# A two-block transformer kernel: the expert router by masking, and half of one small product moved behind the first expert products

## The reference, cut to what matters

```python
def hierarchical_moe(x, w_rg, b_rg, w_re, b_re, w_g, w_u, w_d):
    ...
    g_prob = jax.nn.softmax((xt @ w_rg).astype(jnp.float32) + b_rg.astype(jnp.float32), axis=-1)
    g_val, g_idx = lax.top_k(g_prob, 1)
    e_logit = ((xt @ w_re).astype(jnp.float32) + b_re.astype(jnp.float32)).reshape(n, N_GROUPS, EXPERTS_PER_GROUP)
    e_logit = jnp.take_along_axis(e_logit, g_idx[:, :, None], axis=1)[:, 0]
    e_prob = jax.nn.softmax(e_logit, axis=-1)
    e_val, e_idx = lax.top_k(e_prob, TOP_K_IN_GROUP)
    e_val = e_val / jnp.sum(e_val, axis=-1, keepdims=True)
    within = jnp.sum(jax.nn.one_hot(e_idx, EXPERTS_PER_GROUP, dtype=jnp.float32) * e_val[..., None], axis=1)
    comb = jax.nn.one_hot(g_idx[:, 0], N_GROUPS, dtype=jnp.float32)[:, :, None] * (g_val * within)[:, None, :]
    ...

def second_block(...):
    ...
        x = layer_norm(ALPHA * x + mix, ln1_g[i], ln1_b[i])
        ffn = hierarchical_moe(x, w_route_group[i], b_route_group[i], w_route_expert[i], ...)
        ple = jax.nn.sigmoid(x @ w_ple_gate[i]) * (p[i] @ w_ple[i])
        x = layer_norm(ALPHA * x + ffn + ple, ln2_g[i], ln2_b[i])
```

## Time and profile before

| | us |
|---|---|
| three runs | 1791.07, 1795.44, 1798.85 |
| median | 1795.44 |
| profiled execution, its span | 1793.8 |

### The profile page before, as it was taken

One profiled execution on the slowest core, in us unless ns is written; L12 is line 12 of the kernel. 1 busy time (PEld: TensorE's weight loads), 2 busy tenths in 40 slices (PEclk: granted clock), 3 DMA queues, 4 the chain that ended last, 5 costly groups with the idle time before them and its releaser, 6 DMA issues.

```text
span 1793.8 us, 26178 instructions
## 1 busy us (share of the span) xinstructions
PE 1637.8 (91%) x10696; PEld 1288.2 (72%) x10696; DVE 1084.7 (60%) x1540; ACT 745.7 (42%) x974; POOL 0.2 (0%) x4
## 2 busy tenths in 40 slices
PE   7999999999999999999999899868779989997776
PEld 6877799998877798998887676435368767653433
DVE  6966767877886768877587662221265965412124
ACT  4666444554546535454456541101044564211111
POOL 0000000000000000000000000000000000000000
PEclk9999999999999999999999999989889999899888
DMA  7543346554563445555643499999945427899996
GB/s 257 181 150 135 129 165 203 172 199 148 180 194 102 160 134 188 187 179 153 208 154 122 164 406 381 417 416 414 401 146 181 165 94 289 351 413 416 413 416 240
DMA packets 174272, 422.55 MB, mean 236 GB/s; under 512 B 15984, under 2 KB 68568, under 8 KB 157528
## 3 DMA queue, kind: packets, MB, share of 16 engines
q1 hardware_dynamic: 174168, 421.07, 64.3%
HBM read 419.99 MB, written 1.05 MB: 235 GB/s over the span
## 4 chain that ended last, share of the span: by engine, by line
PE 63%; DMA 15%; DVE 12%; SPq 4%; ACT 3%; issue 3%; DVEq 0%; ACTq 0%
PE lot L287 16%; PE lot L289 16%; PE lot L288 16%; DVE w_lo L257 4%; PE lot L2248 4%; DMA e_hi<-w_exp_up 3%; SPq L2145 3%; DMA two_e_gates<-w_exp_down 3%; DMA raw<-w_exp_up 2%; ACT w_hi L252 2%; DMA two_e_sqT<-w_exp_up 1%; DMA two_e_gates<-w_exp_up 1%; DMA e_lo<-w_exp_up 1%; PE lot L414 1%; DMA e_hi<-w_exp_down 1%
## 5 line engine op out<-in xcount | busy, mean ns | idle before, releaser
L257 DVE TENSOR_TENSOR w_lo<-raw,w_hi 128x2048 fp32r<-128x2048 f32 (+4 forms) x194 | 431.8, 2230 | 129.0 <-ACT w_hi L252 128.3
L252 ACT ACTIVATE w_hi<-raw 128x2048 fp32r<-128x2048 f32 (+4 forms) x194 | 361.5, 1867 | 152.1 <-PE lot L289 138.1
L287 PE MATMUL lot<-one_hT_hi,w_hi 128*128 128x256 f32 x704 | 199.3, 283 | 0.7 <-issue 0.7
L289 PE MATMUL lot<-one_hT_hi,w_lo 128*128 128x256 f32 x704 | 199.2, 283 | 0.0
L288 PE MATMUL lot<-one_hT_lo,w_hi 128*128 128x256 f32 x704 | 199.2, 283 | 0.0
L287 PE MATMUL lot<-w_hi,two_hT_hi 128*128 128x512 f32 (+1 forms) x448 | 178.9, 399 | 4.7 <-DVE two_hT_lo L380 3.1
L289 PE MATMUL lot<-w_hi,two_hT_lo 128*128 128x512 f32 (+1 forms) x448 | 174.0, 388 | 0.0
L288 PE MATMUL lot<-w_lo,two_hT_hi 128*128 128x512 f32 (+1 forms) x448 | 173.9, 388 | 0.0
L287 PE MATMUL lot<-w_hi,one_hT_hi 128*128 128x512 f32 (+2 forms) x384 | 149.3, 389 | 6.9 <-DVE w_lo L257 5.3
L289 PE MATMUL lot<-w_hi,one_hT_lo 128*128 128x512 f32 (+2 forms) x384 | 145.7, 380 | 0.0
L288 PE MATMUL lot<-w_lo,one_hT_hi 128*128 128x512 f32 (+2 forms) x384 | 145.6, 379 | 0.0
(11 more groups left out here) (431 smaller groups left out, 3256.1 us busy)
## 6 DMA issues: line engine op xcount, KB each, us to landing
raw<-w_in SPq DMA_DIRECT2D x78, 1024.0 KB, 5.0
raw<-ffn_w_up SPq DMA_DIRECT2D x44, 1024.0 KB, 5.1
raw<-ffn_w_down SPq DMA_DIRECT2D x22, 1024.0 KB, 5.0
raw<-w_out SPq DMA_DIRECT2D x16, 1024.0 KB, 5.7
raw<-w_exp_gate SPq DMA_DIRECT2D x14, 1024.0 KB, 18.3
raw<-w_exp_up SPq DMA_DIRECT2D x14, 1024.0 KB, 20.6
two_e_gates<-w_exp_up SPq DMA_DIRECT2D x12, 1024.0 KB, 19.3
e_hi<-w_exp_up SPq DMA_DIRECT2D x10, 1024.0 KB, 22.3
```

What stands on the lines that cost most here:

```text
L252: act.activation(K.hi[:, r, 0:n], self.raw(name)[:, 0:n], ACT.Copy).then_inc(K.sig["hi_ready"], 1)
L257: dve.tensor_tensor(K.lo[:, r, 0:n], self.raw(name)[:, 0:n], K.hi[:, r, 0:n].bitcast(F32), ALU.subtract).then_inc(K.sig["lo_ready"], 1)
L287: pe.matmul(out, a[0], b[0], start=start, stop=False)
L289: return pe.matmul(out, a[1], b[0], start=False, stop=stop)
```

## The change

In the router, the two searches within the group go. The group's search stays, but with is-greater as its last step, which marks the three groups that were not picked (`cold`). One step a tile adds -1e30 there to the 32 expert logits. The instruction `max` then gives the eight largest of a tile's 32 values; six of the eight are overwritten by a marker that no value equals, `match_replace` writes the marker over the two that are left, and one comparison with -2e38 gives the marks. The softmax works on 32 values and not on 8. The weights' arithmetic that needed `expert_exps` moves behind `E.rows(dve, 0)`.

On PE, `pl1` is cut by tiles: tile 0 stays ahead of the rank products, tile 1 moves behind the first gate products `E.hidden(pe, 0, 0, 0)`, and the semaphore is raised behind tile 1. On ACT, the copy of `pl1` moves behind the copies of the first gather.

```diff
--- before.py
+++ after.py
@@ -2851,16 +2851,19 @@
         ST.done(out_part(0, 1, 1), "wo01")
         out_part(1, 1, 1).then_inc(L.filled("wot1"), 1)
 
-        def second_products(c):
-            lot = L.claim(pe, f"pl{c}")
+        def second_products(c, tiles=range(T)):
+            lot = L.use[f"pl{c}"][0]
+            if tiles[0] == 0:
+                L.claim(pe, f"pl{c}")
             if c == 0:
                 pe.wait_ge(sig["wple_in"], sig.at("wple_in", 16))
                 both("pT")
-            for t in range(T):
+            for t in tiles:
                 for k in range(2):
                     last = pe.matmul(K.ps[lot][:, t, :], M.pT[:, k, t * P:(t + 1) * P],
                                      w_ple[:, k, c * 512:(c + 1) * 512], start=k == 0, stop=k == 1)
-            last.then_inc(L.filled(f"pl{c}"), 1)
+            if t == T - 1:
+                last.then_inc(L.filled(f"pl{c}"), 1)
 
         def route_tile(t):
 
@@ -2880,7 +2883,7 @@
         route_tile(0)
         transpose_tile(K, L, pe, K.x, "nTt1", 1, sig, "n1_normed")
         route_tile(1)
-        second_products(1)
+        second_products(1, (0,))
         pe.wait_ge(sig["selected"], sig.at("selected", 1))
         L.claim(pe, "rank")
         tri, ones = M.tri_r[:, 0:P], M.tri_r[:, P:2 * P]
@@ -2893,6 +2896,7 @@
         both("rt")
         E.gather(pe, 0)
         E.hidden(pe, 0, 0, 0)
+        second_products(1, (1,))
         both("rank")
         L.claim(pe, "count")
         out = K.ps[L.use["count"][0]]
@@ -3081,9 +3085,9 @@
         act.wait_ge(sig["group_shift"], sig.at("group_shift", 1))
         act.activation(M.r[:, 0, :, 0:N_G], M.r[:, 0, :, 0:N_G], ACT.Exp).then_inc(sig["group_exps"], 1)
         act.wait_ge(sig["expert_shift"], sig.at("expert_shift", 1))
-        act.activation(M.r[:, 3, :, :], M.r[:, 3, :, :], ACT.Exp).then_inc(sig["expert_exps"], 1)
+        act.activation(M.r32[:, :, :], M.r32[:, :, :], ACT.Exp).then_inc(sig["expert_exps"], 1)
+        E.act_pieces(act, 0)
         take("pl1", M.pl[:, 1, :, :], whole)
-        E.act_pieces(act, 0)
         E.silu(act, 0, 0)
         if QB == 1:
             E.act_pieces(act, 1)
@@ -3341,45 +3345,33 @@
            M.route_b[:, :].unsqueeze(1).to_broadcast([P, T, N_ROUTE]), ALU.add).then_inc(L.drained("rt"), 1)
         L.wait_drained(dve, "rt")
 
-        def first_of(out, v, top, index, n):
-
-            small = M.r[:, 7, :, 0:n]
-            link(tt(small, v, top.to_broadcast([P, T, n]), ALU.is_equal))
-            link(dve.scalar_tensor_tensor(small, small, -100.0, index.unsqueeze(1).to_broadcast([P, T, n]),
-                                          ALU.mult, ALU.add))
-            link(dve.tensor_reduce(st[:, 146:148], small, AX_X, ALU.min))
-            link(tt(out, small, st[:, 146:148].unsqueeze(2).to_broadcast([P, T, n]), ALU.is_equal))
-
-        def top_of(cols, v):
-            link(dve.tensor_reduce(st[:, cols], v, AX_X, ALU.max))
-            return st[:, cols].unsqueeze(2)
-
-        g = M.logit[:, :, 0:N_G]
-        hot = M.r[:, 1, :, 0:N_G]
-        top = top_of(slice(140, 142), g)
-        tt(M.r[:, 0, :, 0:N_G], g, top.to_broadcast([P, T, N_G]), ALU.subtract).then_inc(sig["group_shift"], 1)
-        first_of(hot, g, top, M.iota[:, 0:N_G], N_G)
-
-        e = M.logit[:, :, N_G:N_ROUTE].rearrange("p t (g e) -> p t g e", g=N_G)
-        r32 = M.r32[:, :, :].rearrange("p t (g e) -> p t g e", g=N_G)
-        link(tt(r32, e, hot.unsqueeze(3).to_broadcast([P, T, N_G, E_G]), ALU.mult))
-        el, one, two, pe_ = M.r[:, 2, :, :], M.r[:, 4, :, :], M.r[:, 5, :, :], M.r[:, 3, :, :]
-        link(dve.tensor_reduce(el, M.r32[:, :, :].rearrange("p t (g e) -> p t e g", g=N_G), AX_X, ALU.add))
-        top = top_of(slice(142, 144), el)
-        tt(pe_, el, top.to_broadcast([P, T, E_G]), ALU.subtract).then_inc(sig["expert_shift"], 1)
-        first_of(one, el, top, M.iota[:, 4:12], E_G)
-        link(dve.scalar_tensor_tensor(el, one, NEG, el, ALU.mult, ALU.add))
-        top = top_of(slice(144, 146), el)
-        first_of(two, el, top, M.iota[:, 4:12], E_G)
-        link(tt(two, one, two, ALU.add))
-        by_group = lambda m: m.unsqueeze(2).to_broadcast([P, T, N_G, E_G])
-        tt(M.r32_r[:, :, :].rearrange("p t (g e) -> p t g e", g=N_G), hot.unsqueeze(3).to_broadcast([P, T, N_G, E_G]),
-           by_group(two), ALU.mult).then_inc(sig["selected"], 1)
+        by_group = lambda m: m.rearrange("p (g e) -> p g e", g=N_G)
+        g, e = M.logit[:, :, 0:N_G], M.logit[:, :, N_G:N_ROUTE]
+        small, cold = M.r[:, 7, :, 0:N_G], M.r[:, 1, :, 0:N_G]
+        link(dve.tensor_reduce(st[:, 140:142], g, AX_X, ALU.max))
+        top = st[:, 140:142].unsqueeze(2).to_broadcast([P, T, N_G])
+        link(tt(small, g, top, ALU.is_equal))
+        tt(M.r[:, 0, :, 0:N_G], g, top, ALU.subtract).then_inc(sig["group_shift"], 1)
+        link(dve.scalar_tensor_tensor(small, small, -100.0, M.iota[:, 0:N_G].unsqueeze(1).to_broadcast([P, T, N_G]),
+                                      ALU.mult, ALU.add))
+        link(dve.tensor_reduce(st[:, 146:148], small, AX_X, ALU.min))
+        link(tt(cold, small, st[:, 146:148].unsqueeze(2).to_broadcast([P, T, N_G]), ALU.is_gt))
+        for t in range(T):
+            last = dve.scalar_tensor_tensor(by_group(M.r32[:, t, :]), cold[:, t, :].unsqueeze(2).to_broadcast([P, N_G, E_G]),
+                                            NEG, by_group(e[:, t, :]), ALU.mult, ALU.add)
+        link(last)
+        for t in range(T):
+            last = dve.max(M.top8[:, t, :], M.r32[:, t, :])
+        link(last)
+        link(dve.memset(M.top8[:, :, 2:8], PICKED))
+        for t in range(T):
+            last = dve.match_replace(M.w32[:, t, :], M.top8[:, t, :], M.r32[:, t, :], PICKED)
+        link(last)
+        dve.tensor_scalar(M.r32_r[:, :, :], M.w32[:, :, :], -2e38, None, ALU.is_lt).then_inc(sig["selected"], 1)
+        tt(M.r32[:, :, :], M.r32[:, :, :], M.top8[:, :, 0:1].to_broadcast([P, T, N_E]), ALU.subtract)\
+            .then_inc(sig["expert_shift"], 1)
         dve.wait_ge(sig["group_exps"], sig.at("group_exps", 1))
         link(dve.tensor_reduce(st[:, 148:150], M.r[:, 0, :, 0:N_G], AX_X, ALU.add))
-        dve.wait_ge(sig["expert_exps"], sig.at("expert_exps", 1))
-        link(tt(one, two, pe_, ALU.mult))
-        link(dve.tensor_reduce(st[:, 150:152], one, AX_X, ALU.add))
         dve.wait_ge(sig["selected"], sig.at("selected", 1))
         lot = L.wait_filled(dve, "rank")
         tt(M.rank[:, :, :], K.ps[lot][:, 0, 0:T * N_E].rearrange("p (t e) -> p t e", t=T), M.r32_r[:, :, :].bitcast(F32),
@@ -3387,11 +3379,12 @@
             .then_inc(L.drained("rank"), 1)
         L.wait_drained(dve, "rank")
         E.rows(dve, 0)
+        dve.wait_ge(sig["expert_exps"], sig.at("expert_exps", 1))
+        link(tt(M.w32[:, :, :], M.r32[:, :, :], M.r32_r[:, :, :].bitcast(F32), ALU.mult))
+        link(dve.tensor_reduce(st[:, 150:152], M.w32[:, :, :], AX_X, ALU.add))
         link(tt(st[:, 148:150], st[:, 148:150], st[:, 150:152], ALU.mult))
         link(dve.reciprocal(st[:, 148:150], st[:, 148:150]))
-        link(tt(one, one, st[:, 148:150].unsqueeze(2).to_broadcast([P, T, E_G]), ALU.mult))
-        link(tt(M.w32[:, :, :].rearrange("p t (g e) -> p t g e", g=N_G),
-                M.r32_r[:, :, :].bitcast(F32).rearrange("p t (g e) -> p t g e", g=N_G), by_group(one), ALU.mult))
+        link(tt(M.w32[:, :, :], M.w32[:, :, :], st[:, 148:150].unsqueeze(2).to_broadcast([P, T, N_E]), ALU.mult))
         E.weigh_rows(dve, 0)
         E.dve_pieces(dve, 0)
         E.row_weights(dve, 0)
```

## The result

| | before | changed |
|---|---|---|
| median, us | 1795.09 (6 runs) | 1810.07 (6 runs, 1803.7 to 1812.71) |
| span of the profiled execution, us | 1793.8 | 1806.8 |

The ratio is 1.0077, with an interval of 1.0054 to 1.0101: the changed kernel is slower, by 13.8 us of 1795 (the two medians themselves lie 15.0 apart). The forecast was 1808 and its sum +12.7 us on the span; the span grew by 13.0.

A forecast was written before the change was run, and what follows sets the result against it. The prediction took PE to bound the kernel up to the first expert products, then a gapless load stream at 414 GB/s. Late loads +13.6 us less 0.9 gave +12.7 on span 1793.8, 1806.5; median 1808, range 1800 to 1814.

The forecast's parts named there:

- The bound, and the load of G6: Gapless load stream at 414 GB/s; G6, waiting for pl1's moved tail, delays it 5.07 + 1.72 us a layer, 13.6 in both.
- The DVE part: Router on DVE: bias add to marks takes 2.89 us instead of 4.69, between 2.7 and 3.3.
- The PE part: PE ahead of the gather: half of pl1 leaves, so gathers start 1.6 and 2.4 us earlier, 4.0 together.
- The clock: PE's clock stays low 3.4 us longer into each gather, losing 1.3 and 1.8 us; 0.9 of the 4.0 gain is left.
- a sign for both: Sign expected in the new trace: the gather starts 1 to 2.5 us earlier.
- The sum: Whole span: 13.6 - 0.9 = +12.7 us on 1793.8, giving 1806.5; median predicted at 1808.
- What costs nothing: PE's later gate-to-up step (1.72 us), G6's landing, ACT's moved copy and DVE's moved weights add no time.
- the sign that I named: Sign expected in the new trace: PE's first wait for a matrix is longer by about 6 us.
- A gather at full clock (1): Rival on PE's clock: it is not lost in the gathers; 13.6 - 4.0 = +9.6 us, 1805; chance 0.22.
- A gather at half clock to its end, 3.8 us dearer (2): Rival on PE's clock: it stays low through both gathers; 13.6 + 3.6 = +17.2 us, 1812.6; chance 0.10.
- A stream with slack (3): Rival on the load stream: the late G6 vanishes in the queue; 1791.4 to 1794.5 us, not slower; chance 0.06.
- rival 4: Rival: wait not shortened, PE's half product ends last, max and match_replace dearer; +13.5 us, 1809; within the forecast's 0.57.

The follow-up runs named there:

- e3: Kernel before, with only SP's wait changed: the load of G6 waits for the counts product instead of pl1; 1808.13 us, ratio 1.0067.
- e4: Changed kernel, but SP's load of G6 waits only for tile 0 of pl1, tile 1's half reading other data; 1792.87 us, ratio 0.998.
- e2: Kernel before with its old router, only pl1 split and ACT's copy moved as in the changed kernel; 1815.27 us, ratio 1.0103.
- e1: Changed kernel's new router alone, with pl1 whole ahead of the rank products and ACT's order as before; 1795.66 us, ratio 1.0002.
- e9: Arrangement of e7 (pl1 quarters in PE's gaps, ten identity transposes) with the old router of three searches; 1795.13 us, ratio 0.9991.
- e6: Changed kernel with two quarters of pl1 in PE's pauses, the rest ahead of the rank, ACT's copy back in place; 1791.17 us, ratio 0.9968.
- e7: e6 with ten transposes of the identity on PE ahead of the wait for the marks; 1788.95 us, ratio 0.9953.
- e10: The same kernel as e7, run again beside e9 as its comparison; 1788.99 us, ratio 0.9959.

## Why the prediction was right

- **The bound, and the load of G6: right.** 5.07 + 1.72 us a layer was the largest term. The tail of `pl1` took 1.91 (four entries and their start, not 4 x 0.43). With 1.91 the two layers are 14.0 less the 2.4 that the gate products gained, 11.6; the last loads came 12.3 later. e3 shows the term by itself, e4 that nothing is left without it. The Trainium skill (DMA: Bandwidth & Descriptors, "Rules for kernel authors") says, for overlap with compute, to issue the DMA early and wait for it late; this trace agrees: in the first layer 2.10 MB issued 13.0 us later cost the 5.07 us that they had been carried for nothing. The page gives the fixed set-up cost as what overlaps; here it was the bytes.
- **The DVE part: right.** Marks behind the bias add 2.78 us, forecast 2.89; `max` and `match_replace` as read from the slope (0.36 from a pair of `max` to the next start, forecast 0.35; the pair of `match_replace` with its loads 0.45, as forecast).
- **The PE part: right in kind, off in place.** I had PE and DVE level in the first layer and PE last in the second. PE was last in both, by 0.75 us in the first (1074.52 against 1073.77) and 0.46 in the second (1557.18 against 1556.72).
- **The clock: the step that failed, inside a sum that held.** I let it fall when it fell before and stay low for 3.4 us more, a loss of 1.3 and 1.8 us. In the first layer it fell 3.7 us earlier, counted from the transposes, ahead of the changed code. From trace to trace: the router's product of tile 1 cost 1.65 more, the half product 1.64 less than the whole one had, the transposes 0.05 and the rank 0.21 more, the gather 1.77 more: 2.04 later, where I had 0.3 earlier. In the second it was back at 1557.5, before the gather: router product 1.65 and `pl1` 2.76 less, 4.41 earlier, where I had 0.6. The gather thus starts 0.28 us later in the first layer and 4.42 earlier in the second, where I had named 1 to 2.5 earlier as a sign for both. Together 2.4 gained for 0.9 forecast; the error is small in the sum only since the two layers went opposite ways.
- **The sum: partly luck.** With the terms as measured it is 14.0 - 2.4 = +11.6 us, and the span grew by 13.0. Of the 1.4 that are left 0.5 lie ahead of the first transposes; the rest is in none of my terms. That the sum came near rests on the large term; that it came within 0.3 us is chance.
- **What costs nothing: right, but not the sign that I named.** G6 was there in time. PE's first wait for a matrix, though, was 2.11 us and is now 4.17, with 1.70 at the next group, 3.8 longer and not the forecast 6. Before and now, the first of them:

```profile
1114.11 0.60 PE L2248 MATMUL lot<-two_e_gates,two_xw 128*32 128x256 f32 x1 [2.11 <-DMA raw<-w_exp_up]
...
1114.04 0.61 PE L2248 MATMUL lot<-two_e_pt,two_xw 128*32 128x256 f32 x1 [4.17 <-DMA two_e_gates<-w_exp_gate]
```

Nor do later waits make up for the rest. From the last of the first gate products to the same pair of products (L2230) at the end of the first layer's experts, before and now (columns of the earlier trace rows):

```profile
1082.54:1291.04 208.50, 168.03 (x1595) 96.76 (x1595) 46.76 (x84) 24.27 (x36) 0.00 (x0) 0.93 1.02 411
...
1085.08:1300.59 215.51, 173.69 (x1599) 99.76 (x1599) 46.67 (x84) 26.54 (x38) 0.00 (x0) 0.90 1.01 406
```

It is 7.0 us longer, but PE is idle for only 1.35 of these; it is busy for 5.66 more, 1.91 with the moved half of `pl1` (the four entries more) and 3.75 with the same 1595 at a lower clock. So a late stream need not show as long waits of the engine that it feeds. The stream beside them runs at 413 GB/s over the whole stretch, so the slower products do not set the pace.
- **Rivals.** A gather at full clock (1) came true in the second layer. A gather at half clock to its end, 3.8 us dearer (2), came in neither: the first lost 1.77, near the 1.3 of the forecast, and the longest of any profile, e2's 6.44, lost 2.63. A stream with slack (3) is excluded by e3. Of rival 4 PE's half product did end last in both layers, but `max` and `match_replace` were not dearer; its claim that the change doesn't shorten the wait was true of the first layer alone, where the gather starts 0.28 us later because of the clock.

## What to carry to other kernels

When a product is moved behind other work, follow its semaphore to every queue that waits for it, and in a queue that issues in order read all that stands behind the wait. Bytes carried in an idle stretch of DMA ahead of a full stream cost nothing there; when they leave it they are paid at the rate of that stream (here 2.10 MB a layer at 414 GB/s, 5.07 us). A shorter chain on one engine is worth nothing until the engine that ends last is shortened too; here that took cutting `pl1` into the pauses that PE had anyway, and only then did the router's 1.9 us count (e1 and e9, each with one of the two, come to 1.0002 and 0.9991, neither clear of 1; with both it is 0.9953 and 0.9959).

## What the runs showed of the hardware

The moment at which the clock falls is not a property of PE's program alone. e3 has PE's program of before, yet its clock was low for 10.2 us in the first layer (the router's product of tile 1 3.63 us, `pl1` 6.09) and for 3.4 inside `pl1` in the second (1.98 and 5.21); before it was the other way round (1.98 and 5.21, then 3.63 and 6.03). Before, the short case takes 21.96 us from the transposes to D1 and the long one 24.65, so a layer holds some 2.7 us up or down that no reading of one trace can give.

What went with it is how PE was filled ahead of the router. In the eight profiles with pauses of 1.21 and 1.11 us ahead of the router's products, which are 36 columns wide, the clock fell at both routers, for 3.4 to 17.1 us. In the three with 0.34 and 0.25 (e6, e7, e10) it stayed at 2.4 GHz at both, and in e9, which has the same filling but idles 1.91 us ahead of the rank and 0.92 behind it, it fell in both gathers; e6, which idles 1.07 and 0.92 us there, kept it. The Trainium skill (TensorE: Matmul & The Clock Gate, "HAM oscillation — how this bites in real kernels") names long waits for DMA as the cause; here it fell behind pauses of little over 1 us, and these are waits for a copy out of PSUM. e6 changes the length of the pauses and the order of the products together, so which of the two keeps the clock up is not shown, and one profiled execution a kernel doesn't tell how often each case comes.

`max` on 32 elements took 0.29 us for two, `match_replace` 0.17, the load of its values 0.09, and the overwriting of twelve values 0.07, with 0.10 to the next start, where I had 0.19.
